# Experts' up matmuls that alternate between the gate's and the up branch's bank

## The chip, the cores and the metric

The kernel runs on one core of a Trainium2 chip. The metric is the time of one execution on the device in microseconds; lower is better. Matmuls run on TensorE (PE; its weight loads are shown apart as PEld), elementwise work on VectorE (DVE) and ScalarE (ACT), some set-up on GpSimd (POOL), and SyncE (SP) issues nearly all loads from HBM.

## The reference, cut to what matters

Two blocks of two layers each, batch 1, 256 tokens, model width 1024, all in float32. The change touches the mixture of experts in the second layer of the first block: eight experts, each token goes to two.

```python
def moe_swiglu(hn, router, w1, w3, w2):
    bsz, s, d = hn.shape
    t = hn.reshape(-1, d)
    logits = (t @ router).astype(jnp.float32)
    top_vals, top_idx = lax.top_k(logits, TOP_K)
    top_w = jax.nn.softmax(top_vals, axis=-1)
    gates = jnp.sum(top_w[..., None] * jax.nn.one_hot(top_idx, N_EXPERTS, dtype=jnp.float32), axis=1)
    out = jnp.zeros_like(t)
    for e in range(N_EXPERTS):
        h_e = jax.nn.silu(t @ w1[e]) * (t @ w3[e])
        out = out + gates[:, e:e + 1].astype(t.dtype) * (h_e @ w2[e])
    return out.reshape(bsz, s, d)
```

The hidden width of an expert is 3584. The rest of the program is two other feed-forward shapes, mixers, projections and norms, which the change leaves alone.

## The kernel before

Precision: each float32 weight W is split into a rounded part and a remainder, Whi and Wlo, and so is each activation X. A product X W is three matmuls: Xhi Whi, Xhi Wlo, Xlo Whi, summed in PSUM.

The weights stream through rings of six slots of 128 x 1024 numbers (512 KB). A piece of weight that fills one slot is called a chunk here. Its way: SP issues the load into `raw_ring` (L378), ACT casts it to `whi_ring` (L1403, semaphore `hi_ready`), DVE writes raw minus hi to `wlo_ring` (L1966, semaphore `lo_ready`), PE uses it and raises `chunk_used`. SP waits before a load until the chunk six earlier is split (`lo_ready`); ACT waits before a cast for the data (`raw_full`) and until PE has used the chunk six earlier. ACT and DVE work at most three chunks (`LEAD`) ahead of the step of the program at which they stand: `ahead(c)` on either engine does all chunks up to c + 3. Every engine runs its own instructions strictly in the order of the code.

If no expert has more than 128 tokens the sparse form runs, as it does with these inputs. `gather_pair` has put the tokens of an expert into 128 rows, as `xg0hi/lo` or `xg1hi/lo` for two experts each. Each expert's 3584 hidden columns are cut into seven groups of 512, so there are 56 groups G. A group takes 12 chunks: 0 to 3 are w1 (gate), 4 to 7 are w3 (up branch), each with two blocks of 128 rows by 512 columns, and 8 to 11 are w2 (down) of the group before; G = 0 has the first eight alone. PE's order for one group:

- `up_half(G, 0)` (L763): 24 matmuls on chunks 0 to 3 into the gate's bank, with an extra step `aux` after chunk 1 in some groups. An `aux` gathers tokens for the next pair of experts, or combines the last expert's output, in bank 7.
- `turn_hidden(G-1)` (L774): four transposes of the hidden values of the group before into bank 6.
- `up_half(G, 1)`: 24 matmuls on chunks 4 to 7 into the up branch's bank, with an `aux` after chunk 5. Groups use banks 0 and 1, or 2 and 3, by turns.
- `down_group(G-1)` (L789): 24 matmuls on chunks 8 to 11; two in a row have the same stationary block and write banks 4 and 5.

PE waits for `lo_ready` of each chunk ahead of its first matmul. ACT and DVE follow a list of twelve steps i per group (`group(G, i)`, behind `ahead`): ACT does silu of the gate's bank (L1550) at i = 3, and behind it the rounding of the transposed hidden values (`hidden_hi`, L1541); DVE does their remainder (`hidden_lo`, L2140) at i = 3 and the product silu x up branch (L2154) at i = 7, just after the split of chunk 10. At the end of an expert ACT copies the output of the down matmuls (L1559) and DVE takes the remainder (L2159).

Of the kernel before, what the change touches and what calls it, by code (L numbers as in the profile page):

```python
# [16 lines left out]
KT = D // P  # L17
# [36 lines left out]
def build(nc, A, out):  # L54

    ctx = ExitStack()
    with ctx:
# [316 lines left out]
        def _(sp):  # L374
# [16 lines left out]
            for ph in plan:  # L391
# [8 lines left out]
                elif ph["kind"] == "moe":  # L400
                    for G in range(N_GROUPS + 1):
                        e, g = divmod(G, GROUPS)
                        if G < N_GROUPS:
                            for a, w in enumerate((ph["w1"], ph["w3"])):
                                for j in range(4):
                                    c_ = m_chunk(G, 4 * a + j)
                                    src = w[e][2 * j * P:(2 * j + 2) * P, g * GW:(g + 1) * GW]
                                    load(c_, c_ % RING, src.rearrange("(k p) n -> p k n", p=P))
                        if G > 0:
                            e, g = divmod(G - 1, GROUPS)  # L410
                            for j in range(4):
                                c_ = m_chunk(G, (8 if G < N_GROUPS else 0) + j)
                                load(c_, c_ % RING, rows(ph["w2"][e], g * GW + j * P))
# [136 lines left out]
        def _(pe):  # L550
# [89 lines left out]
            def moe_dense():  # L640

                def up(c_, slot, prior):
# [3 lines left out]
                    for i in range(8):  # L646
                        pe.wait_ge(s["lo_ready"], c_ + i + 1)
                        wh, wl = halves(slot + i)
                        for kk in range(2):
                            kt = 2 * (i % 4) + kk  # L650
                            for t in range(TT):
                                ts = slice(t * P, (t + 1) * P)
                                for a, (x, w) in enumerate(((XHI, wh), (XHI, wl), (XLO, wh))):
                                    last = mm(BANK[2 * (i // 4) + t][:, :], x[:, kt, ts], w[:, kk, :],
                                              start=(kt == 0 and a == 0), stop=(kt == KT - 1 and a == 2))
# [44 lines left out]
            def moe_sparse():  # L700
# [43 lines left out]
                def up_half(G, half):  # L744
# [4 lines left out]
                    wait(pe, ("m_silu", "m_hid")[half], G - 1)  # L749
                    if G and G % (2 * GROUPS) == 0 and half == 0:  # L750
                        pe.wait_ge(s["aux_free"], naux[0])
                    bank = BANK[2 * (G % 2) + half]
                    for j in range(4):
                        c_ = m_chunk(G, 4 * half + j)
                        if G == 0 and half == 0:
                            pe.wait_ge(s["xgh_ready"], j + 1)
                            pe.wait_ge(s["xgl_ready"], j + 1)
                        pe.wait_ge(s["lo_ready"], c_ + 1)
                        wh, wl = halves(c_)
                        for kk in range(2):  # L760
                            kt = 2 * j + kk
                            for a, (x, w) in enumerate(((xh, wh), (xh, wl), (xl, wh))):
                                last = mm(bank[:, :], x[:, kt, slots], w[:, kk, :],  # L763
                                          start=(kt == 0 and a == 0), stop=(kt == KT - 1 and a == 2))
                        last.then_inc(s["chunk_used"], 1)
                        if j == 1:
                            aux(G, half)
# [32 lines left out]
                for G in range(N_GROUPS):  # L800
                    up_half(G, 0)
                    if G:
                        turn_hidden(G - 1)
                    up_half(G, 1)
# [587 lines left out]
        def _(act):  # L1392
# [124 lines left out]
            def moe_sparse():  # L1517
# [25 lines left out]
                def group(G, i):  # L1543
# [3 lines left out]
                    if i == 3:  # L1547
                        act.wait_ge(s["chunk_used"], m_chunk(G, 3) + 1)
                        wait(act, "m_hid", G)
                        af(SILG, BANK[2 * (G % 2)][:, :], ACT.Silu).then_inc(s["m_silu"], 1)  # L1550
                        if G:
                            hidden_hi(G - 1)
                    if i == 5:
                        aux(G, 1)
# [397 lines left out]
        def _(dve):  # L1952
# [154 lines left out]
            def moe_sparse():  # L2107
# [35 lines left out]
                def group(G, i):  # L2143
# [7 lines left out]
                    if i == 7:  # L2151
# [776 lines left out]
```

## Time and profile before

| | us |
|---|---|
| median of three runs | 2645.59 |
| lowest, highest | 2645.48, 2647.7 |
| span of the profiled execution | 2645.1 |
| PE busy | 2569.9 |
| DVE busy | 1914.2 |
| ACT busy | 1464.1 |
| first and last up matmul of the experts (starts) | 502.3, 1476.3 |

The profile has for each instruction its line, engine, tiles, start and length. A matmul's own length (0.39 us for 512 columns) includes its way through the array; the next starts before it ends, so the pitch from start to start tells what a matmul costs. In a timeline an "x5" row is five instructions in a row, with the time from the first start to the last end; what stands in brackets is how long the engine sat idle before and what ended it.

### The profile page before, as it was taken

Reading aid. Unit: us, or ns where it says so; the run is one execution under the profiler, and the core shown is the slowest. Engines: PE = TensorE matmul, PEld = TensorE weight load, DVE = VectorE, ACT = ScalarE, POOL = GpSimd, SP = SyncE. Lnnn points to the kernel's source line nnn. Section 1 sums busy time; section 2 is a strip of 40 time slices with the busy share of each in tenths; the row PEclk is TensorE's granted clock in tenths of the full one; section 3 lists DMA queues with packets and bytes.
Section 4 is the critical chain, followed back from the end, with each engine's and each line's share of the span. In section 5 each row is a group of like instructions: output and inputs, shape, how many; then the busy total and the mean of one; then the engine's idle time right before and its main releaser. Section 6 shows DMA issues by size and latency. Waiting matters only on the chain.

```text
span 2645.1 us, 41339 instructions
## 1 busy us (share of the span) xinstructions
PE 2569.9 (97%) x15616; PEld 2260.2 (85%) x15616; DVE 1914.2 (72%) x2596; ACT 1464.1 (55%) x1870; POOL 64.5 (2%) x137
## 2 busy tenths in 40 slices
PE   9999999899999999999999999999999999999998
PEld 8699987788888888888888799898899999898997
DVE  5565565689898989889999855688655655797554
ACT  5444353577777777777777634532533534524433
POOL 7000000000000000000000000000000000000000
PEclk9899999999999999999999999999999999999999
DMA  7255643499999999999999865422565565413562
GB/s 206 80 165 186 183 136 123 151 364 363 346 356 366 355 350 358 366 354 352 358 365 362 271 194 182 145 81 80 177 190 184 158 187 181 125 57 104 183 189 96
DMA packets 481895, 597.26 MB, mean 226 GB/s; under 512 B 21882, under 2 KB 313154, under 8 KB 481760
## 3 DMA queue, kind: packets, MB, share of 16 engines
q1 hardware_dynamic: 478048, 589.47, 66.1%
q0 software_dynamic: 3712, 6.00, 0.8%
q8 instruction: 83, 1.36, 0.2%
q14 instruction: 52, 0.43, 0.0%
HBM read 594.35 MB, written 1.05 MB: 225 GB/s over the span
## 4 chain that ended last, share of the span: by engine, by line
PE 88%; DVE 8%; ACT 2%; issue 1%; DMA 0%; SPq 0%; DVEq 0%; ACTq 0%
PE bank L601 24%; PE bank L763 24%; PE bank L789 12%; PE bank L613 11%; PE bank L585 4%; PE bank L582 2%; DVE arena L2663 1%; PE bank L1351 1%; DVE wlo_ring L1966 1%; PE bank L904 1%; PE bank L774 1%; PE bank L1073 1%; PE bank L819 1%; PE bank L825 1%; PE bank L710 1%
## 5 line engine op out<-in xcount | busy, mean ns | idle before, releaser
L1966 DVE TENSOR_TENSOR wlo_ring<-raw_ring,whi_ring 128x1024 fp32r<-128x1024 f32 (+1 forms) x1122 | 1317.9, 1218 | 127.1 <-ACT whi_ring L1403 118.3
L1403 ACT CAST whi_ring<-raw_ring 128x1024 fp32r<-128x1024 f32 (+1 forms) x1122 | 1139.2, 1053 | 201.1 <-DMA raw_ring<-in_od_exp_w_dram 148.3
L601 PE MATMUL bank<-xhi,whi_ring 128*128 128x256 f32 x1760 | 498.8, 283 | 1.0 <-DVE xlo L2023 1.0
L601 PE MATMUL bank<-xlo,whi_ring 128*128 128x256 f32 x1760 | 498.0, 283 | 0.0
L601 PE MATMUL bank<-xhi,wlo_ring 128*128 128x256 f32 x1760 | 498.0, 283 | 0.0
L601 PEld LDWEIGHTS bank<-xhi,whi_ring 128*128 128x128 f32 x1760 | 337.2, 192 | 5.7 <-issue 1.8
L601 PEld LDWEIGHTS bank<-xlo,whi_ring 128*128 128x128 f32 x1760 | 337.3, 192 | 3.9
L2041 DVE TENSOR_TENSOR hid<-sil,bank 128x256 f32<-128x256 f32 x110 | 46.3, 421 | 402.4 <-ACT sil L1454 402.4
L601 PEld LDWEIGHTS bank<-xhi,wlo_ring 128*128 128x128 f32 x1760 | 337.3, 192 | 0.0
L1454 ACT ACTIVATE sil<-bank 128x256 f32<-128x256 f32 x110 | 42.3, 385 | 499.1 <-PE bank L601 499.1
L763 PE MATMUL bank<-whi_ring,xg0hi 128*128 128x512 f32 x448 | 180.4, 403 | 0.7 <-issue 0.7
L763 PE MATMUL bank<-whi_ring,xg1hi 128*128 128x512 f32 x448 | 179.9, 401 | 0.0
L763 PE MATMUL bank<-whi_ring,xg1lo 128*128 128x512 f32 x448 | 177.3, 396 | 0.0
L763 PE MATMUL bank<-whi_ring,xg0lo 128*128 128x512 f32 x448 | 177.3, 396 | 0.0
L763 PE MATMUL bank<-wlo_ring,xg1hi 128*128 128x512 f32 x448 | 177.2, 395 | 0.0
L763 PE MATMUL bank<-wlo_ring,xg0hi 128*128 128x512 f32 x448 | 177.1, 395 | 0.0
L585 PE MATMUL bank<-xhi,whi_ring 128*128 128x256 f32 (+1 forms) x512 | 152.0, 297 | 1.4 <-DVE xlo L2023 1.4
L585 PE MATMUL bank<-xlo,whi_ring 128*128 128x256 f32 (+1 forms) x512 | 145.7, 284 | 0.0
L585 PE MATMUL bank<-xhi,wlo_ring 128*128 128x256 f32 (+1 forms) x512 | 145.6, 284 | 0.0
L789 PE MATMUL bank<-whi_ring,hidhi 128*128 128x512 f32 x448 | 139.2, 392 | 1.4 <-DVE hidlo L2140 1.4
L789 PE MATMUL bank<-whi_ring,hidlo 128*128 128x512 f32 x448 | 138.4, 390 | 0.0
L789 PE MATMUL bank<-wlo_ring,hidhi 128*128 128x512 f32 x448 | 138.0, 389 | 0.0
(504 smaller groups left out, 3826.0 us busy)
## 6 DMA issues: line engine op xcount, KB each, us to landing
raw_ring<-in_od_exp_w_dram SPq DMA_DIRECT2D x672, 512.0 KB, 5.4
raw_ring<-in_ffn_w_gate_dram SPq DMA_DIRECT2D x88, 512.0 KB, 3.9
raw_ring<-in_ffn_w_up_dram SPq DMA_DIRECT2D x88, 512.0 KB, 5.3
raw_ring<-in_ffn_w_down_dram SPq DMA_DIRECT2D x88, 512.0 KB, 5.2
raw_ring<-in_ev_ffn_w_dram SPq DMA_DIRECT2D x66, 512.0 KB, 4.9
raw_ring<-in_w_in_dram SPq DMA_DIRECT2D x42, 512.0 KB, 4.1
raw_ring<-in_od_w_in_dram SPq DMA_DIRECT2D x24, 512.0 KB, 3.8
raw_ring<-in_ev_w_in_dram SPq DMA_DIRECT2D x20, 512.0 KB, 6.6
```

Source lines behind the costliest of these rows:

```text
L582: last = mm(banks[t] if banks else row_bank(q, n, t), x[:, kt, t * P:(t + 1) * P], w[:, kk, :], start=st and (n > 256 or t == 0), stop=sp_ ...
L585: last = mm(BANK[q % 2][0:n, 0:S], w[:, kk, :], x[:, kt, :], start=st, stop=sp_)
L601: last = mm(BANK[qb][:, half * S:half * S + n], w[:, kt, :], x, start=(kt == 0 and a == 0), stop=(kt == KT - 1 and a == 2))
L613: last = mm(pair[h][:, :], x[:, b, t * P:(t + 1) * P], w[:, h * 512:(h + 1) * 512], start=(start and a == 0), stop=(stop and a == 2), skip ...
L710: last = mm(bank[:, q * S:(q + 1) * S], src[:, t, kt * P:(kt + 1) * P], PSEL[:, t, 2 * p:2 * p + 2, :].rearrange("p a b -> p (a b)"), star ...
L763: last = mm(bank[:, :], x[:, kt, slots], w[:, kk, :], start=(kt == 0 and a == 0), stop=(kt == KT - 1 and a == 2))
L774: last = tr(BANK[6][:, j * P:(j + 1) * P], HIDG[:, j * P:(j + 1) * P], IDENT[:, :])
L789: last = mm(BANK[4 + h][:, :], x[:, j * P:(j + 1) * P], w[:, h * 512:(h + 1) * 512], start=(g == 0 and j == 0 and a == 0), stop=(g == GROU ...
L1403: nc.scalar.copy(WHI[:, slot, 0:n], RAW[:, slot, 0:n]).then_inc(s["hi_ready"], 1)
L1454: af(SIL[:, b, 0:n], BANK[b][:, 0:n], ACT.Silu).then_inc(s["silu_ready"], 1)
L1966: V_.tensor_tensor(WLO[:, slot, 0:n], RAW[:, slot, 0:n], WHI[:, slot, 0:n].bitcast(F32), ALU.subtract)\
L2041: V_.tensor_tensor(HID[:, b, 0:n], SIL[:, qb, 0:n], BANK[qb][:, S:S + n], ALU.mult)\
```

## The change

SP loads the chunks of w1 and w3 by turns: chunk 2j is the gate's j-th, chunk 2j + 1 the up branch's j-th. PE works through a group in four quarters (`up_quarter(G, j)`, L764 and L765 in the changed file), each on two chunks. A matmul for the gate's bank and one for the up branch's bank follow each other with the same stationary block of x. A quarter waits for both its chunks at once and marks both used at its end. The extra steps stand after quarters 0 and 2, the transposes after quarter 1. Silu on ACT goes from i = 3 to i = 7, `hidden_hi` stays at i = 3, the product on DVE goes from i = 7 to i = 8. The dense form of the experts, which doesn't run with these inputs, gets the same order of chunks.

```diff
--- before.py
+++ after.py
@@ -401,9 +401,9 @@
                     for G in range(N_GROUPS + 1):
                         e, g = divmod(G, GROUPS)
                         if G < N_GROUPS:
-                            for a, w in enumerate((ph["w1"], ph["w3"])):
-                                for j in range(4):
-                                    c_ = m_chunk(G, 4 * a + j)
+                            for j in range(4):
+                                for a, w in enumerate((ph["w1"], ph["w3"])):
+                                    c_ = m_chunk(G, 2 * j + a)
                                     src = w[e][2 * j * P:(2 * j + 2) * P, g * GW:(g + 1) * GW]
                                     load(c_, c_ % RING, src.rearrange("(k p) n -> p k n", p=P))
                         if G > 0:
@@ -647,11 +647,11 @@
                         pe.wait_ge(s["lo_ready"], c_ + i + 1)
                         wh, wl = halves(slot + i)
                         for kk in range(2):
-                            kt = 2 * (i % 4) + kk
+                            kt = 2 * (i // 2) + kk
                             for t in range(TT):
                                 ts = slice(t * P, (t + 1) * P)
                                 for a, (x, w) in enumerate(((XHI, wh), (XHI, wl), (XLO, wh))):
-                                    last = mm(BANK[2 * (i // 4) + t][:, :], x[:, kt, ts], w[:, kk, :],
+                                    last = mm(BANK[2 * (i % 2) + t][:, :], x[:, kt, ts], w[:, kk, :],
                                               start=(kt == 0 and a == 0), stop=(kt == KT - 1 and a == 2))
                         last.then_inc(s["chunk_used"], 1)
 
@@ -741,30 +741,30 @@
                     last.then_inc(s["aux_mm"], 1)
                     naux[0] += 1
 
-                def up_half(G, half):
+                def up_quarter(G, j):
 
                     e = G // GROUPS
                     xh, xl = XG[(e // 2) % 2]
                     slots = slice((e % 2) * P, (e % 2 + 1) * P)
-                    wait(pe, ("m_silu", "m_hid")[half], G - 1)
-                    if G and G % (2 * GROUPS) == 0 and half == 0:
-                        pe.wait_ge(s["aux_free"], naux[0])
-                    bank = BANK[2 * (G % 2) + half]
-                    for j in range(4):
-                        c_ = m_chunk(G, 4 * half + j)
-                        if G == 0 and half == 0:
-                            pe.wait_ge(s["xgh_ready"], j + 1)
-                            pe.wait_ge(s["xgl_ready"], j + 1)
-                        pe.wait_ge(s["lo_ready"], c_ + 1)
-                        wh, wl = halves(c_)
-                        for kk in range(2):
-                            kt = 2 * j + kk
-                            for a, (x, w) in enumerate(((xh, wh), (xh, wl), (xl, wh))):
-                                last = mm(bank[:, :], x[:, kt, slots], w[:, kk, :],
-                                          start=(kt == 0 and a == 0), stop=(kt == KT - 1 and a == 2))
-                        last.then_inc(s["chunk_used"], 1)
-                        if j == 1:
-                            aux(G, half)
+                    if j == 0:
+                        wait(pe, "m_hid", G - 1)
+                        if G and G % (2 * GROUPS) == 0:
+                            pe.wait_ge(s["aux_free"], naux[0])
+                    if G == 0:
+                        pe.wait_ge(s["xgh_ready"], max(j + 1, 2))
+                        pe.wait_ge(s["xgl_ready"], j + 1)
+                    pair = BANK[2 * (G % 2)], BANK[2 * (G % 2) + 1]
+                    c_ = m_chunk(G, 2 * j)
+                    pe.wait_ge(s["lo_ready"], c_ + 2)
+                    (w1h, w1l), (w3h, w3l) = halves(c_), halves(c_ + 1)
+                    for kk in range(2):
+                        kt = 2 * j + kk
+                        for a, (x, w1, w3) in enumerate(((xh, w1h, w3h), (xh, w1l, w3l), (xl, w1h, w3h))):
+                            st, sp_ = (kt == 0 and a == 0), (kt == KT - 1 and a == 2)
+                            gate = mm(pair[0][:, :], x[:, kt, slots], w1[:, kk, :], start=st, stop=sp_)
+                            up_ = mm(pair[1][:, :], x[:, kt, slots], w3[:, kk, :], start=st, stop=sp_)
+                    gate.then_inc(s["chunk_used"], 1)
+                    up_.then_inc(s["chunk_used"], 1)
 
                 def turn_hidden(G):
 
@@ -798,10 +798,14 @@
                         pe.wait_ge(s["hnl_ready"], TT)
                     gather_pair(BANK[u], 0, u).then_inc(s["first_gath"], 1)
                 for G in range(N_GROUPS):
-                    up_half(G, 0)
+                    up_quarter(G, 0)
+                    aux(G, 0)
+                    up_quarter(G, 1)
                     if G:
                         turn_hidden(G - 1)
-                    up_half(G, 1)
+                    up_quarter(G, 2)
+                    aux(G, 1)
+                    up_quarter(G, 3)
                     if G:
                         down_group(G - 1, m_chunk(G, 8))
                 turn_hidden(N_GROUPS - 1)
@@ -1544,14 +1548,14 @@
 
                     if i == 1:
                         aux(G, 0)
-                    if i == 3:
-                        act.wait_ge(s["chunk_used"], m_chunk(G, 3) + 1)
+                    if i == 3 and G:
+                        hidden_hi(G - 1)
+                    if i == 5:
+                        aux(G, 1)
+                    if i == 7:
+                        act.wait_ge(s["chunk_used"], m_chunk(G, 7) + 1)
                         wait(act, "m_hid", G)
                         af(SILG, BANK[2 * (G % 2)][:, :], ACT.Silu).then_inc(s["m_silu"], 1)
-                        if G:
-                            hidden_hi(G - 1)
-                    if i == 5:
-                        aux(G, 1)
 
                 def expert_out(e, used):
                     act.wait_ge(s["chunk_used"], used)
@@ -2148,7 +2152,7 @@
                         hidden_lo(G - 1)
                     if i == 5:
                         aux(G, 1)
-                    if i == 7:
+                    if i == (8 if G else 7):
                         dve.wait_ge(s["m_silu"], G + 1)
                         dve.wait_ge(s["chunk_used"], m_chunk(G, 7) + 1)
                         V_.tensor_tensor(HIDG, SILG, BANK[2 * (G % 2) + 1][:, :], ALU.mult).then_inc(s["m_hid"], 1)
```

PE at the first up matmuls of a group, before: one bank, three products after each other, a wait for each chunk (6 matmuls).

```order
L763 MATMUL bank<-whi_ring,xg1hi 128x512 [waits lo_ready,aux_free,m_silu]
L763 MATMUL bank<-wlo_ring,xg1hi 128x512
L763 MATMUL bank<-whi_ring,xg1lo 128x512
L763 MATMUL bank<-whi_ring,xg1hi 128x512
L763 MATMUL bank<-wlo_ring,xg1hi 128x512
L763 MATMUL bank<-whi_ring,xg1lo 128x512
L763 MATMUL bank<-whi_ring,xg1hi 128x512 [waits lo_ready]
```

After: gate (L764) and up branch (L765) by turns, the next wait comes after twelve matmuls (the last row here).

```order
L764 MATMUL bank<-whi_ring,xg1hi 128x512 [waits lo_ready,aux_free,m_hid]
L765 MATMUL bank<-whi_ring,xg1hi 128x512
L764 MATMUL bank<-wlo_ring,xg1hi 128x512
L765 MATMUL bank<-wlo_ring,xg1hi 128x512
L764 MATMUL bank<-whi_ring,xg1lo 128x512
L765 MATMUL bank<-whi_ring,xg1lo 128x512
...
L764 MATMUL bank<-whi_ring,xg1hi 128x512 [waits lo_ready]
```

What moved: each product of the gate has its partner of the up branch behind it, and every second wait for `lo_ready` is gone, the ones left being for two chunks.

ACT in one group, from the casts ahead of i = 3 to the casts behind i = 7, before:

```order
L1403 CAST whi_ring<-raw_ring 128x1024 [waits chunk_used,raw_full3]
L1403 CAST whi_ring<-raw_ring 128x1024 [waits chunk_used,raw_full4]
L1550 ACTIVATE sil<-bank 128x512 [waits m_hid,chunk_used]
L1541 CAST hidhi<-bank 128x512 [waits m_tp]
L1403 CAST whi_ring<-raw_ring 128x1024 [waits chunk_used,raw_full5]
L1403 CAST whi_ring<-raw_ring 128x1024 [waits chunk_used,raw_full0]
L1403 CAST whi_ring<-raw_ring 128x1024 [waits chunk_used,raw_full1]
```

After:

```order
L1407 CAST whi_ring<-raw_ring 128x1024 [waits chunk_used,raw_full3]
L1407 CAST whi_ring<-raw_ring 128x1024 [waits chunk_used,raw_full4]
L1545 CAST hidhi<-bank 128x512 [waits m_tp]
L1407 CAST whi_ring<-raw_ring 128x1024 [waits chunk_used,raw_full5]
L1407 CAST whi_ring<-raw_ring 128x1024 [waits chunk_used,raw_full0]
L1407 CAST whi_ring<-raw_ring 128x1024 [waits chunk_used,raw_full1]
L1407 CAST whi_ring<-raw_ring 128x1024 [waits chunk_used,raw_full2]
L1558 ACTIVATE sil<-bank 128x512 [waits m_hid,chunk_used]
L1407 CAST whi_ring<-raw_ring 128x1024 [waits chunk_used,raw_full3]
L1407 CAST whi_ring<-raw_ring 128x1024 [waits chunk_used,raw_full4]
L1407 CAST whi_ring<-raw_ring 128x1024 [waits chunk_used,raw_full5]
```

Silu left its place ahead of the rounding of the hidden values and stands four casts further down, behind the cast of chunk 10 and in front of that of chunk 11.

DVE from the remainder of the hidden values to the end of an expert, before:

```order
L2140 TENSOR_TENSOR hidlo<-bank,hidhi 128x512 [waits m_hidhi]
L1966 TENSOR_TENSOR wlo_ring<-raw_ring,whi_ring 128x1024 [waits hi_ready] x4
L2154 TENSOR_TENSOR hid<-sil,bank 128x512 [waits chunk_used,m_silu]
L1966 TENSOR_TENSOR wlo_ring<-raw_ring,whi_ring 128x1024 [waits hi_ready] x4
L2159 TENSOR_TENSOR yel<-bank,yeh 128x512 [waits yeh_ready] x2
```

After:

```order
L2144 TENSOR_TENSOR hidlo<-bank,hidhi 128x512 [waits m_hidhi]
L1970 TENSOR_TENSOR wlo_ring<-raw_ring,whi_ring 128x1024 [waits hi_ready] x5
L2158 TENSOR_TENSOR hid<-sil,bank 128x512 [waits chunk_used,m_silu]
L1970 TENSOR_TENSOR wlo_ring<-raw_ring,whi_ring 128x1024 [waits hi_ready] x3
L2163 TENSOR_TENSOR yel<-bank,yeh 128x512 [waits yeh_ready] x2
```

The product stands one split later, behind that of chunk 11.

## Rows read from the trace of the kernel before

**Rows 1.** The page's first lines: span, then busy us, share, instructions
```profile
span 2645.1 us, 41339 instructions
...
PE 2569.9 (97%) x15616; PEld 2260.2 (85%) x15616; DVE 1914.2 (72%) x2596; ACT 1464.1 (55%) x1870; POOL 64.5 (2%) x137
```

**Rows 2.** Busy us (and instructions) of each engine, clock, DMA share, 600 to 1400 us
```profile
600.00:1400.00 800.00, 800.00 (x3595) 652.72 (x3594) 723.35 (x688) 608.25 (x661) 0.00 (x0) 1.00 0.99 357
```

**Rows 3.** Waits from 520 to 1480 us: total us, times, longest
```profile
ACT whi_ring L1403 <- DMA raw_ring<-in_od_exp_w_dram: 148.0, 312, 1.8
ACT sil L1550 <- PE bank L763: 50.9, 52, 2.0
...
PEld bank L763 <- DVE wlo_ring L1966: 0.4, 1, 0.4
```

**Rows 4.** Timeline of PE across one group: start us, us, instruction
```profile
871.27 0.60 PE L774 MATMUL bank<-ident,hid 128*128 128x128 f32 x4
871.63 0.48 PE L763 MATMUL bank<-whi_ring,xg1hi 128*128 128x512 f32 x1
871.95 0.39 PE L763 MATMUL bank<-wlo_ring,xg1hi 128*128 128x512 f32 x1
...
877.09 0.39 PE L763 MATMUL bank<-whi_ring,xg1lo 128*128 128x512 f32 x1
877.32 0.63 PE L789 MATMUL bank<-whi_ring,hidhi 128*128 128x512 f32 x2
...
880.08 0.61 PE L789 MATMUL bank<-whi_ring,hidhi 128*128 128x512 f32 x2
...
881.44 0.61 PE L789 MATMUL bank<-whi_ring,hidhi 128*128 128x512 f32 x2
...
882.80 0.39 PE L763 MATMUL bank<-whi_ring,xg1hi 128*128 128x512 f32 x1
```

**Rows 5.** Timeline of ACT, same stretch
```profile
871.47 0.60 ACT L1550 ACTIVATE sil<-bank 128x512 f32<-128x512 f32 x1 [0.68 <-PE bank L763]
871.97 0.58 ACT L1541 CAST hidhi<-bank 128x512 fp32r<-128x512 f32 x1
872.43 4.85 ACT L1403 CAST whi_ring<-raw_ring 128x1024 fp32r<-128x1024 f32 x5
...
883.00 1.08 ACT L1559 CAST yeh<-bank 128x512 fp32r<-128x512 f32 x2 [1.13 <-PE bank L789]
883.96 1.07 ACT L1403 CAST whi_ring<-raw_ring 128x1024 fp32r<-128x1024 f32 x1
```

**Rows 6.** Timeline of DVE, same stretch
```profile
873.53 4.63 DVE L1966 TENSOR_TENSOR wlo_ring<-raw_ring,whi_ring 128x1024 fp32r<-128x1024 f32 x4 [0.26 <-ACT whi_ring L1403]
878.08 0.68 DVE L2154 TENSOR_TENSOR hid<-sil,bank 128x512 f32<-128x512 f32 x1
878.68 4.62 DVE L1966 TENSOR_TENSOR wlo_ring<-raw_ring,whi_ring 128x1024 fp32r<-128x1024 f32 x4
883.62 1.29 DVE L2159 TENSOR_TENSOR yel<-bank,yeh 128x512 fp32r<-128x512 f32 x2 [0.32 <-ACT yeh L1559]
```

**Rows 7.** Timeline of PE in a projection (L582) and at an extra step (L710)
```profile
384.29 0.39 PE L582 MATMUL bank<-whi_ring,xhi 128*128 128x512 f32 x1
384.52 0.39 PE L582 MATMUL bank<-whi_ring,xlo 128*128 128x512 f32 x1
384.75 0.39 PE L582 MATMUL bank<-wlo_ring,xhi 128*128 128x512 f32 x1
384.97 0.39 PE L582 MATMUL bank<-whi_ring,xhi 128*128 128x512 f32 x1
...
1205.06 0.64 PE L710 MATMUL bank<-psel,xlo 128*128 128x256 f32 x4
1205.53 0.39 PE L763 MATMUL bank<-whi_ring,xg0hi 128*128 128x512 f32 x1
```

## Prediction, made before the changed kernel ran

> **What bounds the kernel now.** I read the page first: TensorE (PE) is busy 97% of a span of 2645.1 us [rows 1]. The table by stretches shows that the sparse experts, from 502 to 1490 us, are the densest part: in 600 to 1400 us PE is busy 800.00 of 800.00 us at full clock, VectorE (DVE) 90%, ScalarE (ACT) 76%, and the DMA engines 99% at 357 GB/s [rows 2]. The list of waits of that stretch says who is late: ACT waits 148.0 us for raw chunks and 50.9 us for PE, PE waits once, 0.4 us, for a split chunk [rows 3]. So PE alone sets the time there. Every ns off a matmul's pitch counts in full, and every stall of PE adds in full. There are 56 groups with 48 up matmuls each, 2688 in all.
>
> Below, chunks 0 to 7 are a group's up chunks, 8 to 11 the down chunks of the group before, 0' and 1' the next group's first two. E is the end of the last up matmul of a group: 877.09 + 0.39 = 877.48 us in the rows. X is the end of the four transposes: 871.27 + 0.60 = 871.87 us [rows 4].
>
> **The pitch (a gain).** Up matmuls start 0.2336 us apart (22 of them from 871.95 to 877.09). Down matmuls have the same shape, come in pairs with one stationary block and alternate between two banks: 24 take 877.32 to 882.80, 0.2283 each over all 24, and 0.2267 once steady (880.08 to 881.44 for six) [rows 4]. The new up matmuls are written exactly like the down ones. The bounds are zero and 6.9 ns for each matmul (0.2336 - 0.2267), so 0 to 18.5 us. I take the average over all 24 of a down group, since the new order also restarts PE several times a group: 5.3 ns x 2688 = 14 us.
>
> Against it speaks the projection before: three matmuls in a row there write one bank with a changing stationary block, and they start 0.227 us apart, 384.29 to 384.97 [rows 7]. So one bank three times costs nothing; whether twenty-four times does, no row shows. The Trainium skill (TensorE: Matmul & The Clock Gate, Back-to-back issue gap) gives a gap that depends on the moving columns alone, N/2.4 + 2.5 ns or about 216 ns; our two lines with 512 columns each differ by 5 to 7 ns, so the trace does not agree. By the page's rule, which has no term for the bank, the gain would be zero, which is a rival below.
>
> **The price: PE wants two chunks where it wanted one.** A quarter starts only when both its chunks are split; the second was wanted six matmuls (1.4 us) later before. Who makes them is a chain of ACT casts (one each 0.95 us, the last 1.05: five take 4.85) [rows 5] and DVE splits (one each 1.137, the last 1.22: four take 4.63) [rows 6]. At two places per group this chain cannot start before PE reaches a point, because ACT has to serve PE first.
>
> *Place B, after the last up matmul.* Silu moves from the middle of the group to E, in front of the cast of chunk 11 on ACT; behind it are queued the casts of 11, 0', 1'. From E: silu starts at +0.04, the next ACT instruction 0.49 later (871.47 to 871.97 [rows 5]), so the cast of 11 runs +0.54 to +1.59. DVE splits 11 from +1.62; the product of silu and up branch now stands behind it and occupies 0.60 before the next split (878.08 to 878.68 [rows 6]); so it starts at +2.76, the split of 0' at +3.36, that of 1' at +4.50, done at +5.72. The raw data are there: ACT was free at that place and had long cast chunk 10. In the kernel before the next group's first matmul starts at 882.80, which is E + 5.32, after 24 down matmuls that don't change [rows 4]. Now it needs 1' and starts at about +5.77: 0.45 late. A restart costs 0.085 more, since the first interval after a gap is 0.32 instead of 0.2336 (871.63 to 871.95 [rows 4]). 0.53 x 55 groups = 29 us.
>
> *Place A, after the transposes.* ACT's cast of hidden values waits for X, and the cast of chunk 7 is queued behind it. It starts at X + 0.05, chunk 7's cast at +0.52 (0.47 later, rows 871.97 and 872.43 [rows 5]), to +1.58; the split from +1.61 to +2.83. This chain is as before; the need is not. The third quarter starts at X - 0.24 (871.63) and lasts 0.085 + 12 x 0.2283, so the fourth, which wants chunk 7 at once, is due at X + 2.59. It starts at about +2.86: 0.27 late, with the restart 0.36. Where an extra step of PE (gathers, combines) lies between, it covers 0.47 (1205.06 to 1205.53 [rows 7]): 28 groups have one there, and I count 0.05 each (1.4 us). The other 27 (the first group has no transposes) pay 0.36: 10 us.
>
> *Place C, the seven ends of an expert.* ACT waits for the last down matmul and makes two copies (883.00, next cast 0.96 later), DVE two subtractions (1.29) [rows 5, 6], all ahead of chunk 3'. From E: copies at +5.52, cast of 3' +6.48 to +7.54, subtractions +6.8 to +8.1, split of 3' to about +9.2. The second quarter is due at 5.77 + 0.085 + 2.74 + 0.47 (a combine) = +9.07. 0.2 late and a restart: 2 us in seven.
>
> Sum of the stalls: 29 + 10 + 1.4 + 2 = 42. The Trainium skill (Perfetto Trace Analysis, Matmuls) speaks against this change: groups should rotate through banks so that the evacuation of one overlaps the next one's matmuls. The trace agrees, since silu ran at 871.47 while PE went on with the up branch until E; with both banks finished together nothing of the up work is left to cover it, and by that rule the evacuation (0.60 of silu and 0.68 of product in the rows) has to be hidden by the down matmuls alone, which is place B.
>
> The other edits cost nothing: the number of instructions, bytes and chunks is unchanged; the loads follow the new order of use; the extra steps stay after two of eight chunks; the transposes stay after four, and the hidden values of the group before are ready at E + 3.4, long before them.
>
> **Sum.** 2645.1 + 42 - 14 = 2673 us of span; the median of the runs lies 0.5 above the span: 2674. Own range 2662 to 2682, from the upper pitch gain with somewhat smaller stalls to a gain of a third.
>
> **Rivals.**
> 1. *Stalls, but no pitch gain.* For it: the projection's same-bank matmuls at 0.227. Against: the down matmuls run beside the same traffic and are faster. With a slower third quarter place A falls to 0.29 x 27 = 8: 2645.6 + 40 = 2686.
> 2. *The cover holds: faster.* The 24 down matmuls last 5.48 us; if chunk 1' is split before its weight load is due, 0.22 ahead of the matmul (E + 5.10 instead of my 5.72), place B is empty, and a like 0.3 empties A. It decides at that point. For it: chunks are now ready 1 us and more ahead of PE, and PE waited only 0.4 us [rows 3]. Against: each step of the chain has its row, and none can shrink by 0.6. It gives 2645.6 - 14 = 2631.
> 3. *Half the stalls,* because one of the two places is empty: 42 falls to about 20, and with the gain of 14 to 18 the time is 2648 to 2651, near no change.
> 4. *Loads fall behind too.* A load waits for the split of the chunk six before; splits come up to 1 us later, and the DMA engines are at 99% [rows 2]. If chunks 5' to 7' land later than ACT wants them, a third stall of about 0.5 comes into each group: + 28, 2702.
>
> **How the numbers follow.** Forecast 0.47; rival 1 0.22; rival 2 0.15; rival 3 0.08; rival 4 0.08. The range must hold 0.8: it takes in the forecast, rival 1, and rival 3: 2646 to 2694. Outside are rival 2 and most of rival 4. A measurement of this kernel tells 0.2% (5.3 us) from no change: faster is below 2640.3, slower above 2650.9. Faster 0.15; rival 3 splits between same (0.07) and slower (0.01), a little of the forecast is same: same 0.08, slower 0.77.
>
> **What the changed profile would show.** PE's up matmuls 0.227 to 0.229 apart, else the first term is zero. A new wait of PE's weight load for DVE's split of about 40 us in all, in some 80 places: 55 at a group's first up matmul, 27 at the fourth quarter. ACT's silu waiting for PE once a group at E, and DVE's product right behind the split of chunk 11. PE's share in 600 to 1400 us falls from 100% to about 97%. If the list of waits has no such entry, my chain is wrong, and rival 2 holds.

## The result, and the profile after

| | median us | runs |
|---|---|---|
| before | 2646.49 | 4 (2645.48 to 2647.7) |
| changed | 2690.71 | 4 (2686.32 to 2693.77) |

The ratio is 1.0167, with a 95% interval of 1.0152 to 1.0181: the change makes the kernel 1.7% slower, by 44 us. The forecast was 2674, with a range of 2646 to 2694. The time lies inside the range, but 17 us above the forecast and 5 from the 2686 of rival 1, stalls without a pitch gain. The range held it because it had been drawn wide enough to take in that rival.

The page's first lines, which answer to [rows 1]: the span grew by 47.0 us, PE's busy time by 21.5.

```profile
span 2692.1 us, 41285 instructions
...
PE 2591.4 (96%) x15616; PEld 2253.1 (84%) x15616; DVE 1912.3 (71%) x2596; ACT 1453.9 (54%) x1870; POOL 63.9 (2%) x137
```

The stretch from 600 to 1400 us, which answers to [rows 2] (busy us of PE, PEld, DVE, ACT, POOL with counts, clock, DMA share, GB/s). PE was busy all 800 us before. Now it is idle for 18.36, at the same full clock, and DVE, ACT and DMA have all fallen with it; none of them became a bound by its amount of work.

```profile
600.00:1400.00 800.00, 781.64 (x3443) 619.72 (x3442) 689.60 (x657) 575.38 (x633) 0.00 (x0) 1.00 0.97 342
```

The waits from 520 to 1520 us, which answer to [rows 3] (total us, times, longest). Before, PE waited once. Now its weight load waits at 88 places: 54 under "issue", all at a group's first up matmul (the entry of 20.7 us is the matmul at these places), and 34 for a split, 27 of them at a fourth quarter and 7 at a second one. ACT's silu waits for PE once a group at the end of the up work. The waits of PE and of PEld lie side by side and are not added.

```profile
ACT whi_ring L1407 <- DMA raw_ring<-in_od_exp_w_dram: 86.3, 173, 1.7
ACT sil L1558 <- PE bank L765: 74.0, 54, 1.7
PEld bank L764 <- issue: 41.9, 54, 0.8
...
PE bank L764 <- DVE wlo_ring L1970: 20.7, 54, 0.4
PEld bank L764 <- DVE wlo_ring L1970: 15.9, 34, 0.5
```

The same group as in [rows 4] (L764 gate, L765 up branch, L774 transposes, L789 down), first PE:

```profile
889.11 0.60 PE L774 MATMUL bank<-ident,hid 128*128 128x128 f32 x4
889.46 0.48 PE L764 MATMUL bank<-whi_ring,xg1hi 128*128 128x512 f32 x1
889.78 0.39 PE L765 MATMUL bank<-whi_ring,xg1hi 128*128 128x512 f32 x1
...
892.11 0.40 PE L765 MATMUL bank<-whi_ring,xg1lo 128*128 128x512 f32 x1
892.59 0.50 PE L764 MATMUL bank<-whi_ring,xg1hi 128*128 128x512 f32 x1
...
895.26 0.39 PE L765 MATMUL bank<-whi_ring,xg1lo 128*128 128x512 f32 x1
895.49 0.63 PE L789 MATMUL bank<-whi_ring,hidhi 128*128 128x512 f32 x2
...
900.51 0.61 PE L789 MATMUL bank<-whi_ring,hidlo 128*128 128x512 f32 x2
901.50 0.47 PE L764 MATMUL bank<-whi_ring,xg1hi 128*128 128x512 f32 x1 [0.38 <-DVE wlo_ring L1970]
901.81 0.40 PE L765 MATMUL bank<-whi_ring,xg1hi 128*128 128x512 f32 x1
```

X is 889.11 + 0.60 = 889.71, E is 895.26 + 0.39 = 895.65. Three things can be read here. From 889.78 to 892.11 there are ten intervals of 0.233: **the pitch has not moved**. The third quarter's last matmul starts at 892.11, the next is due at 892.34 and starts at 892.59: **place A**, 0.25 late. The down matmuls end with a pair at 900.51 and 900.74, the next is due at 900.96 and starts at 901.50: **place B**, 0.54 late; and the interval behind it is 0.31. E to the next group's start was 5.32 us and is 5.85.

The weight load (PEld) ahead of that start:

```profile
901.47 0.19 PEld L764 LDWEIGHTS bank<-whi_ring,xg1hi 128*128 128x128 f32 x1 [0.78 <-issue]
```

ACT and DVE, which answer to [rows 5] and [rows 6]:

```profile
889.75 0.59 ACT L1545 CAST hidhi<-bank 128x512 fp32r<-128x512 f32 x1 [1.78 <-PE bank L774]
890.23 3.89 ACT L1407 CAST whi_ring<-raw_ring 128x1024 fp32r<-128x1024 f32 x4
895.69 0.60 ACT L1558 ACTIVATE sil<-bank 128x512 f32<-128x512 f32 x1 [1.57 <-PE bank L765]
896.19 4.08 ACT L1407 CAST whi_ring<-raw_ring 128x1024 fp32r<-128x1024 f32 x4
```

```profile
891.31 4.63 DVE L1970 TENSOR_TENSOR wlo_ring<-raw_ring,whi_ring 128x1024 fp32r<-128x1024 f32 x4 [0.25 <-ACT whi_ring L1407]
897.26 1.23 DVE L1970 TENSOR_TENSOR wlo_ring<-raw_ring,whi_ring 128x1024 fp32r<-128x1024 f32 x1 [1.32 <-ACT whi_ring L1407]
898.40 0.68 DVE L2158 TENSOR_TENSOR hid<-sil,bank 128x512 f32<-128x512 f32 x1
899.00 3.49 DVE L1970 TENSOR_TENSOR wlo_ring<-raw_ring,whi_ring 128x1024 fp32r<-128x1024 f32 x3
```

This is the chain of the prediction: silu at E + 0.04, the cast of chunk 11 at E + 0.54, its split at E + 1.61, the product at E + 2.75, the split of 0' at E + 3.35, that of 1' from 899.00 + 1.137 to 901.36, which is E + 5.71 (forecast 5.72). The loads are not late: ACT goes from cast to cast.

Over the whole of the experts' stretch (first up matmul to last down matmul) the time grew from 987.0 to 1030.5 us, 43.5 of the 44 to 47. A third place shows in the group behind each end of an expert (**place C**). In the second quarter that follows this same stretch, behind a combine (L719, L720), PE's rows are:

```profile
904.62 0.40 PE L720 MATMUL bank<-yel,pselt 128*128 128x512 f32 x1
904.88 0.51 PE L764 MATMUL bank<-whi_ring,xg1hi 128*128 128x512 f32 x1
905.22 0.40 PE L765 MATMUL bank<-whi_ring,xg1hi 128*128 128x512 f32 x1
```

In the kernel before these two steps are 0.23 and 0.23; here they are 0.26 and 0.34.

Added up from the starts of PE's matmuls, each against its like in the kernel before:

- Place B: the 54 steps from a down matmul to a group's first up matmul take 41.6 us where they took 12.3 (29.3 us, 0.54 each). The interval behind each is longer by 0.079 (4.3 us).
- Place A: the 27 starts of a fourth quarter without an extra step come 0.24 late (6.6 us), and the interval behind each is longer by 0.103 (2.8 us).
- Place C: seven starts come 0.03 late, and the interval behind each is longer by 0.106 (1.0 us).

That is 44.0 us, for a stretch that grew by 43.5.

### The profile page after: what moved, and what is told of

It reads as the page before. It is cut to its first block, busy times and chain, and to the rows that moved or that the text cites. A ratio compares the mean times of both kernels' runs of the same rounds, so it can differ in the third digit from the quotient of the medians.

```text
span 2692.1 us, 41285 instructions
## 1 busy us (share of the span) xinstructions
PE 2591.4 (96%) x15616; PEld 2253.1 (84%) x15616; DVE 1912.3 (71%) x2596; ACT 1453.9 (54%) x1870; POOL 63.9 (2%) x137
## 4 chain that ended last, share of the span: by engine, by line
PE 78%; DVE 16%; ACT 3%; issue 3%; DMA 0%; SPq 0%; ACTq 0%; DVEq 0%
PE bank L601 24%; PE bank L764 11%; PE bank L613 11%; PE bank L765 10%; DVE wlo_ring L1970 7%; PE bank L789 5%; PE bank L585 4%; PE bank L582 2%; ACT whi_ring L1407 2%; DVE arena L2667 2%; DVE hid L2158 1%; PE bank L1355 1%; PE bank L908 1%; PE bank L774 1%; PE bank L1077 1%
## 5 line engine op out<-in xcount | busy, mean ns | idle before, releaser
L789 PE MATMUL bank<-whi_ring,hidhi 128*128 128x512 f32 x448 | 138.8, 391 | 1.6 <-DVE hidlo L2144 1.6
L789 PE MATMUL bank<-wlo_ring,hidhi 128*128 128x512 f32 x448 | 138.2, 390 | 0.0
L789 PE MATMUL bank<-whi_ring,hidlo 128*128 128x512 f32 x448 | 138.1, 389 | 0.0
L613 PE MATMUL bank<-whi_ring,hidhi 128*128 128x512 f32 x440 | 137.1, 393 | 0.0
L613 PE MATMUL bank<-wlo_ring,hidhi 128*128 128x512 f32 x440 | 136.3, 391 | 0.0
L613 PE MATMUL bank<-whi_ring,hidlo 128*128 128x512 f32 x440 | 135.9, 390 | 0.0
L764 PE MATMUL bank<-whi_ring,xg1hi 128*128 128x512 f32 x224 | 95.5, 426 | 12.0 <-DVE wlo_ring L1970 10.7
L764 PE MATMUL bank<-whi_ring,xg0hi 128*128 128x512 f32 x224 | 95.1, 424 | 11.1 <-DVE wlo_ring L1970 10.0
L585 PEld LDWEIGHTS bank<-xhi,whi_ring 128*128 128x128 f32 (+1 forms) x512 | 97.4, 190 | 8.7 <-issue 5.6
```

What stands on the lines that cost most here:

```text
L585: last = mm(BANK[q % 2][0:n, 0:S], w[:, kk, :], x[:, kt, :], start=st, stop=sp_)
L613: last = mm(pair[h][:, :], x[:, b, t * P:(t + 1) * P], w[:, h * 512:(h + 1) * 512], start=(start and a == 0), stop=(stop and a == 2), skip ...
L764: gate = mm(pair[0][:, :], x[:, kt, slots], w1[:, kk, :], start=st, stop=sp_)
L789: last = mm(BANK[4 + h][:, :], x[:, j * P:(j + 1) * P], w[:, h * 512:(h + 1) * 512], start=(g == 0 and j == 0 and a == 0), stop=(g == GROU ...
```

## The experiments

In all of them "pitch" is the mean distance between the starts of neighbouring 512-column matmuls of a line (L764 and L765 taken as one), where it is below 0.3 us, over some 2,400 pairs for the up matmuls: 0.2339 in the kernel before, 0.2339 in the changed one. The medians of before beside them were 2647 to 2649 us. The experts' stretch (first up matmul to last down matmul, in the profiled run) is given where it tells more than the median, since the part of the program ahead of it, the same in all these kernels, took 500.8 us in one profiled run and 510.9 in another. It is 987.0 us before and 1030.5 in the changed kernel.

### Is it the queue on ACT? Silu behind the cast of chunk 11, hidden values behind chunk 7

```diff
 def group(G, i):            # ACT, changed kernel
-    if i == 3 and G:
+    if i == 4 and G:
         hidden_hi(G - 1)
-    if i == 7:
+    if i == (8 if G else 7):
         ... silu ...
 def group(G, i):            # DVE
-    if i == 3 and G:
+    if i == 4 and G:
         hidden_lo(G - 1)
```

> The changed kernel with two moves on ACT and DVE: silu one step later (behind the cast of chunk 11 instead of ahead of it), and the rounding of the hidden values and its remainder one step later (behind chunk 7 instead of ahead of it). PE's order is untouched. Chain theory: at E the casts of chunks 0' and 1' start 0.95 us sooner and the split of 11 is already done, so the split of 1' ends near E + 4.0 and place B (0.53 x 55 = 29 us) is empty; chunk 7 no longer waits for the transposes, so place A (about 10 us) is empty too. Time 2646 to 2652 us, PE's waits for splits under 5 us in all. Rival (the pairing itself costs PE, or loads fall behind): stays above 2675 us.

Measured: 2651.46 us, ratio to before 1.0007 (0.9995 to 1.0018). The pairing, the order of chunks and PE's order are those of the changed kernel, and nearly all of the 44 us is gone; the experts' stretch is 990.4 us, 3.4 above before. ACT and DVE at the same group:

```profile
871.62 0.58 ACT L1545 CAST hidhi<-bank 128x512 fp32r<-128x512 f32 x1 [1.42 <-PE bank L774]
872.11 4.14 ACT L1407 CAST whi_ring<-raw_ring 128x1024 fp32r<-128x1024 f32 x4
877.23 0.60 ACT L1558 ACTIVATE sil<-bank 128x512 f32<-128x512 f32 x1 [0.98 <-PE bank L765]
877.73 2.94 ACT L1407 CAST whi_ring<-raw_ring 128x1024 fp32r<-128x1024 f32 x3
```

```profile
877.86 0.69 DVE L2158 TENSOR_TENSOR hid<-sil,bank 128x512 f32<-128x512 f32 x1
878.80 3.50 DVE L1970 TENSOR_TENSOR wlo_ring<-raw_ring,whi_ring 128x1024 fp32r<-128x1024 f32 x3 [0.25 <-ACT whi_ring L1407]
```

E is 877.19 here. The casts of 0' and 1' are the first of the three behind silu, the split of 1' ends at 878.80 + 1.137 + 1.22 = 881.16, E + 3.97 (expected 4.0), and the next up matmul starts at 882.51, E + 5.32 as before. What is left of PE's waits for splits:

```profile
PEld bank L764 <- DVE wlo_ring L1970: 3.9, 8, 0.5
...
PEld bank L764 <- issue: 2.0, 8, 0.3
```

Seven of the eight places of the first entry are place C, which has grown. PE at the second quarter behind the same end of an expert, and its weight load:

```profile
885.55 0.39 PE L720 MATMUL bank<-yel,pselt 128*128 128x512 f32 x1
886.05 0.50 PE L764 MATMUL bank<-whi_ring,xg1hi 128*128 128x512 f32 x1
886.38 0.39 PE L765 MATMUL bank<-whi_ring,xg1hi 128*128 128x512 f32 x1
```

```profile
886.05 0.19 PEld L764 LDWEIGHTS bank<-whi_ring,xg1hi 128*128 128x128 f32 x1 [0.53 <-DVE wlo_ring L1970]
```

The start is 0.27 late in each of the seven, and with the longer interval behind it this makes 2.6 of the 3.4 us. So the two queue places carried nearly the whole loss (the run moved both at once; how it divides between them is read from the trace of the changed kernel). What the pairs cost beyond them is about 3 us, most of it where ACT and DVE have the output of an expert to copy first.

### Is the late silu enough? Single waits

The changed kernel's chunk order, late silu and late product, with PE taking one chunk at a time:

```diff
-    pe.wait_ge(s["lo_ready"], c_ + 2)
-    ... gate and up branch by turns, twelve matmuls ...
+    for a_ in range(2):
+        c_ = m_chunk(G, 2 * j + a_)
+        pe.wait_ge(s["lo_ready"], c_ + 1)
+        ... six matmuls of this chunk into BANK[2 * (G % 2) + a_] ...
```

> The changed kernel's order of chunks, its late silu and late product, but PE takes one chunk at a time again: six matmuls on the gate's chunk into the gate's bank, then six on the up branch's chunk into the other, with a wait each. Chain theory: the split of 1' still ends at E + 5.7, but is wanted only at E + 6.7, and chunk 7 only 1.4 us later than with pairs, so no stall: 2645 to 2650 us. Rival (the late silu alone costs the time): about 2685 us. On the pitch: if a change of bank every six matmuls were enough, it would fall from 0.234 to 0.227 and the time to about 2630.

Measured: 2646.39 us, ratio 0.9996 (0.9981 to 1.0011), pitch 0.2339; PE has no entry of waiting for a split under the up matmuls. The experts' stretch is 988.7 us, 1.7 above before. The late silu alone costs next to nothing. The loss needs both: a second chunk that comes late, and a step that wants it 1.4 us sooner. A bank that changes every six matmuls does nothing for the pitch, and in the changed kernel one that changes at every matmul did nothing either.

### Where does the pitch come from? The bank's number, and the place of the stationary block

The kernel before with banks 0 to 3 and 4 to 7 exchanged in the sparse experts:

```diff
 def moe_sparse():           # on PE, ACT and DVE
+    BANK = [BANK_ALL[(i + 4) % 8] for i in range(8)]
```

> The kernel before with banks 0 to 3 and 4 to 7 exchanged in the sparse experts, so up matmuls write banks 4 to 7 and down matmuls 0 and 1. If the pitch hangs on the bank's number, up goes to 0.227 and down to 0.234: 2646 - 18 + 9 = 2637. If not, nothing changes: 2646.

Measured: 2646.79 us, ratio 0.9990 (0.9978 to 1.0002), pitch of the up matmuls 0.2339, of the down ones 0.2281 as before. The bank's number is out.

The kernel before with another stationary block. It leaves out the gathered tokens of the expert, so its output is not that of the reference, and it serves for the time alone:

```diff
-    xh, xl = XG[(e // 2) % 2]
+    xh, xl = XHI, XLO
```

> The kernel before with the stationary block of the up matmuls read from the tiles xhi and xlo in place of xg; the numbers are then not the tokens of the expert, all else stays. If the 0.234 us pitch comes from where the stationary block lies, it falls to 0.227 and the time by up to 18 us to about 2628; if it has another cause, 0.234 and 2646.

Measured: 2636.25 us, ratio 0.9941 (0.9916 to 0.9966), and the pitch fell to 0.2280. The same 24 matmuls in one bank, the same order of the three products, the same moving blocks. That ends both readings of the change's idea, alternate banks and shared stationary blocks: **the pitch hangs on the tile from which the weight load reads.** The experts' stretch is 972.2 us.

### What is it about the tile? Its start address

Adding up the tiles in front of it, `xg` starts at byte 137,824 of a partition in the kernel before, 32 past a multiple of 64 and 96 past one of 256. `xhi` (73,728) and `hidhi` (100,352) start on multiples of 1024. Six runs move tiles:

```diff
-        over = [MOE_OVER]
+        over = [MOE_OVER + 8]     # 16, 40, 104 in the others; numbers of 4 bytes
```

```diff
+        PAD8 = sb("pad8", [P, 8])             # boundary_exchanged
         HIDHI = sb("hidhi", [P, 2, S], F32R)
```

```diff
-        STAT = sb("stat", [P, 84])            # arena_on_64_bytes
+        STAT = sb("stat", [P, 92])
```

> The kernel before with the tiles of the sparse experts (xg first among them) moved by 8 numbers, 32 bytes, in each partition. Adding up the tiles ahead of them, xg starts 32 bytes past a multiple of 64 in the kernel before, while xhi, xlo, hidhi and hidlo start on one. If that is the cause of the 0.234 us pitch, the up matmuls come 0.227 to 0.228 apart and the time is 2646 - 16 to 18 = about 2630. If it is the neighbourhood in memory or the way xg is written, nothing changes: 0.234, 2646.

> The same with 16 numbers, 64 bytes: xg is still 32 bytes past a multiple of 64. By the boundary theory the pitch stays 0.234 and the time 2646; if any move helps (another cause than the boundary), it falls as in the run before.

> The kernel before with a pad of 32 bytes ahead of hidhi: hidhi and hidlo, the stationary blocks of all down matmuls (L789 and L613), now start 32 bytes past a multiple of 64, and xg on one. Boundary theory: up 0.227, both down lines 0.234; 2688 matmuls gain and 2664 lose some 6 ns, the time stays within 3 us of 2646. Other causes: down stays 0.227.

> The kernel before with the tile stat 32 bytes longer, so that the whole arena behind it, xg in it, starts on a multiple of 64, and hidhi stays on one. Boundary theory: 16 to 18 us from the up matmuls and perhaps 1 to 3 from the mixers' matmuls out of the arena: 2627 to 2631, faster than both kernels. Otherwise 2646.

The first guess, a boundary of 64 bytes, was wrong in size: 2644.49 us in place of 2630 (ratio 0.9991, 0.9981 to 1.0001), and the same median with the whole arena moved. The pitch had gone down, by 1.2 ns. But `boundary_exchanged` showed that the address matters elsewhere too. There the down matmuls, which had 0.2280 in the experts and 0.2290 in the dense layers, went to 0.2332 and 0.2327. The padding stands ahead of `xg` too, so its start moved by 32 bytes as well, and the up pitch is 0.2324. The rings with the moving blocks lie ahead of it and stayed. The median is 2652.79 (ratio 1.0020, 0.9999 to 1.0042), some 5 us above before, which by the interval is not clear of noise; the pitch is. Two rows of its down matmuls, with 22 intervals between their starts, 5.12 us or 0.2327 each:

```profile
879.90 0.62 PE L790 MATMUL bank<-whi_ring,hidhi 128*128 128x512 f32 x2
...
885.02 0.63 PE L790 MATMUL bank<-whi_ring,hidlo 128*128 128x512 f32 x2
```

So two more moves, to coarser boundaries, against the rival that the region of the memory decides:

> The kernel before with the tiles of the sparse experts moved by 104 numbers, so that xg starts on a multiple of 512 bytes, as xhi and hidhi do. The multiple of 128 reached by a move of 32 bytes took only 1.2 ns off the pitch. If a coarser boundary is the rest of the cause (a block is 128 numbers, 512 bytes), the pitch is 0.227 to 0.228 and the time about 2630. If the region of the memory decides (xg lies above 131072 bytes in the partition, xhi and hidhi below), the pitch stays at 0.232 to 0.233 and the time near 2644.

> The same with 40 numbers: xg starts on a multiple of 256 but not of 512. By the theory of the coarser boundary 256 gives either the whole effect (0.227) or none beyond 128 (0.2326); by that of the region 0.232 to 0.233.

| run | start of xg is a multiple of | up pitch | experts' stretch, us | median us | ratio (interval) |
|---|---|---|---|---|---|
| before | 32 | 0.2339 | 987.0 | 2646 to 2649 | 1 |
| xg_moved_64_bytes | 32 | 0.2335 | 986.3 | 2647.43 | 1.0004 (0.9990 to 1.0018) |
| xg_moved_32_bytes | 128 | 0.2327 | 983.3 | 2644.49 | 0.9991 (0.9981 to 1.0001) |
| arena_on_64_bytes | 128 | 0.2327 | 983.3 | 2644.49 | 0.9991 (0.9979 to 1.0004) |
| xg_on_256_bytes | 256 | 0.2278 | 969.9 | 2629.03 | 0.9927 (0.9905 to 0.9948) |
| xg_on_512_bytes | 512 | 0.2278 | 970.2 | 2630.49 | 0.9926 (0.9898 to 0.9954) |

A multiple of 256 bytes gives the whole effect, and the region is out, since the tile has hardly moved. This kernel is 0.7% faster than the one before, with one number changed, and so faster than the changed one too. Its PE timeline: 22 intervals of down matmuls from 870.26 to 875.25, 0.2268 each, and eleven of up matmuls from 875.70 to 878.20, 0.2273 each.

```profile
870.26 0.62 PE L789 MATMUL bank<-whi_ring,hidhi 128*128 128x512 f32 x2
...
875.25 0.61 PE L789 MATMUL bank<-whi_ring,hidlo 128*128 128x512 f32 x2
875.70 0.39 PE L763 MATMUL bank<-whi_ring,xg1hi 128*128 128x512 f32 x1
...
878.20 0.39 PE L763 MATMUL bank<-whi_ring,xg1lo 128*128 128x512 f32 x1
```

And its stretch from 600 to 1400 us, with 363 GB/s where there were 357 and 342:

```profile
600.00:1400.00 800.00, 799.57 (x3657) 662.87 (x3656) 735.23 (x700) 622.43 (x672) 0.00 (x0) 1.00 0.99 363
```

### The change, and its repaired form, with an aligned xg

> The changed kernel with xg on a multiple of 256 bytes. This is the prediction's own sum with the pitch gain it assumed: the up matmuls 0.227 to 0.228 apart, stalls of about 44 to 48 us as before or slightly more (a faster third quarter uncovers place A by another 0.07 us), so about 2690 - 16 + 2 = 2676 us. If pairing or alternating banks has an effect of its own on an aligned xg, the pitch lies off 0.228.

Measured: 2681.18 us (2676.57 to 2682.12), ratio 1.0130 (1.0113 to 1.0147). The pitch is 0.2291 and the stalls have stayed, 0.57 each at place B. The 5 us above the expected 2676 are in part this pitch: behind every restart it takes about ten intervals to come down to 0.227. In the third quarter, behind the transposes, the means over the groups are 0.316, then 0.233, 0.235, 0.232, 0.229, 0.231, 0.231, 0.228, 0.229, 0.229, 0.227; the stalls add such restarts.

```profile
PEld bank L764 <- issue: 43.1, 54, 0.8
...
PE bank L764 <- DVE wlo_ring L1970: 22.4, 55, 0.5
PEld bank L764 <- DVE wlo_ring L1970: 17.5, 34, 1.0
```

> The changed kernel with silu and the hidden values' rounding out of the way of the casts and xg on a multiple of 256 bytes: no stalls and the fast pitch. About 2630 to 2635 us, like the kernel before with xg on 256 (2629) or some us above it, since pairs want their chunks earlier and the splits have now less time per group. A clear gain over it would need something of the pairing that has not shown so far.

Measured: 2639.21 us (2631.44 to 2644.43), ratio 0.9958 (0.9942 to 0.9975), pitch 0.2280. That is above the 2629 of the unpaired kernel with the same move; the two ratios' intervals, 0.9942 to 0.9975 and 0.9905 to 0.9948, overlap only at their ends. The experts' stretch is 975.5 us against 969.9. Pairing brings nothing on an aligned tile, and since pairs want their chunks sooner, waits for splits remain (5.4 us over nine places, seven of them place C).

## Why the prediction was right and where it was wrong

- **PE alone sets the time, a stall adds in full:** right. PE's late starts, added up one by one, make 44.0 us where the stretch grew by 43.5.
- **The step that failed is the pitch.** The prediction took 14 us for it, on the ground that the new up matmuls are written like the down ones. The pitch was 0.2339 before and after, so this term was zero. The up and the down lines differed in one more thing that neither the code's shape nor the order shows, the start address of the stationary tile, and that is what made the 6 ns. The evidence against the gain was on the table: the projection's matmuls at 0.227 in one bank [rows 7]. They read `xhi`. They had been set aside for being three in a row and not twenty-four, when they were the counterexample to the bank.
- **The average of the down matmuls** was read as if their slow start were a restart. It is not: there is no gap ahead of them. Over the 56 groups their first eight intervals have a mean of 0.2309 and all later ones 0.2267. With xg on 256 bytes they run at 0.2266 to 0.2269 from the second interval on, though their own tile has not moved. So the first down matmuls carried some of the slow pitch of the up matmuls ahead of them; why, no run shows.
- **The rule on the gap** of the Trainium skill (TensorE: Matmul & The Clock Gate, Back-to-back issue gap), N/2.4 + 2.5, counts the moving columns alone. For the change this came out: no gain from the banks. For `xg` it did not: at the same 512 columns the runs show 0.2339 and 0.2278. The page calls its 216 ns the gap of an isolated matmul, which the prediction left out, and gives about 131 ns for a sustained stream; neither was seen, the fastest steady pitch was 0.227.
- **Place B** was forecast at 0.45 late and 0.085 for the restart, 29 us. It is 0.54 and 0.079: 34 us, in 54 groups and not 55, since no down matmuls stand ahead of the second group. The split ends at E + 5.71 as forecast; the first matmul starts 0.14 behind that end (901.36 to 901.50), where 0.05 had been assumed. The weight load's row names "issue", its start is 901.47, so 0.11 of this passes before the load begins.
- **Place A** was forecast at 0.27 late, and 0.2 in rival 1. It is 0.24 in 27 groups, with restarts 9 us. Here the 0.05 behind the split's end was right. The 28 groups with an extra step there lose nothing, where 1.4 us had been set.
- **Place C** is there, at half its size: seven starts 0.03 late and longer intervals behind them, 1.0 us where 2 had been set.
- **Stalls in sum:** 42 forecast, 44 measured. That the sum is so close is in part luck: place B came out 5 us larger, the other places 3 smaller. The 17 us between 2674 and 2690.71 are the 14 us of the pitch, and the rest is within the runs' own spread of 7 us. The number was held by the range, but the forecast's own story, a gain beside the stalls, did not happen; rival 1's did.
- **Rival 2** (the cover holds) has its first half, the empty places A and B, in the kernel that `late_silu_no_queue` made by taking away what the prediction had named, the queue on ACT; the pitch gain of its 2631 never came. **Rival 4** (loads fall behind) didn't come: ACT's waits for raw chunks fell from 148 to 86 us.

## What to carry to other kernels

Where an engine in order serves both the stream of weights and the results of the bound engine, count for every chunk when it is wanted and when the chain behind the last sync can deliver it; wanting two at once took 1.4 us off a cover of about 1 us (the split of 1' ends at E + 5.7, and with single waits and the late silu it is wanted at E + 6.7). The repair is to put the sync behind the work that doesn't need it, here one cast at each of two places. And before a difference in pitch is put down to order or banks, compare the start addresses of the stationary tiles: the one-number move was worth 0.7%, the rewrite cost 1.7%, and repaired it gave nothing.

## What the runs showed of the hardware

- The pitch of 512-column float32r matmuls, each with its own weight load, depends on where the stationary tile starts in its partition: 0.2335 to 0.2339 us at an odd multiple of 32 bytes, 0.2327 at a multiple of 128, 0.2278 at 256 and 512. For `hidhi` and `hidlo` moved by 32 bytes from a multiple of 1024: 0.2280 to 0.2332 in the experts, and 0.2290 to 0.2327 in the dense layers. Blocks of 512 bytes were read from all of them. Why this is so no run here shows. The length of the weight load in the trace doesn't tell it: for the up matmuls its mean is 0.188 us in every run.
- The moving tiles stood still in all these runs, so whether the stationary tile's own address counts or its distance from the moving one is open. Other widths were not tried either, nor an odd multiple of 64.
- Neither the bank's number, nor a bank that alternates with every matmul or every six, nor a stationary block that is the same twice in a row changed the pitch by more than 0.1 ns with xg where it was. On 256 bytes it was 0.2280 with pairs and few stalls, and 0.2278 without pairs.
- A wait that PE really sat out cost, from the end of the releasing split on DVE to the start of the matmul, 0.146 us at the 54 waits of place B and 0.055 at the 34 waits of places A and C, the same to 0.002 within each kind; in `late_silu_no_queue` it is 0.056 at place C, where the wait is 0.27. What makes the difference no run shows. The interval behind the wait is 0.31 us at place B and 0.34 at A and C, where it was 0.23 to 0.24 before.
